# Feed-forward blocks: gated tiles turned by VectorE in 32x32 blocks, and the last down unit's low part formed by GpSimd

## The reference, cut to what matters

```python
def swiglu(x, w1, w3, w2):
    return (jax.nn.silu(x @ w1) * (x @ w3)) @ w2      # inner width 2816
```

## Time and profile before

| what | value |
|---|---|
| time, median of 3 runs | 1487.77 us (1487.43 to 1488.27) |
| profiled execution | span 1485.5 us; with what lies around it the program takes 1487.77 us in the runs above |
| TensorE busy | 1466.1 us, 99% |
| VectorE busy | 865.5 us, 58% |
| ScalarE busy | 687.0 us, 46% |
| GpSimd busy | 184.2 us, 12% |
| TensorE clock | 0.999 of full speed (mean) |

### The profile page before, as it was taken

How to read it: one execution, slowest core, us unless ns; L and a number is a source line. 1 busy time by engine, 2 the same in 40 slices (tenths; PEclk the granted TensorE clock), 3 DMA queues, 4 the chain that set the end, 5 groups by cost and what they waited for, 6 DMA issues and landing times.

```text
span 1485.5 us, 20418 instructions
## 1 busy us (share of the span) xinstructions
PE 1466.1 (99%) x7688; PEld 1237.8 (83%) x7688; DVE 865.5 (58%) x1030; ACT 687.0 (46%) x854; POOL 184.2 (12%) x184
## 2 busy tenths in 40 slices
PE   9999999999999999999999999999999999999998
PEld 8988897888888888889988888888888897788886
DVE  5765756554455545657665544675455677664545
ACT  5346446434444443453434344364434378444342
POOL 1073112000000000300040000300000325500001
PEclk9999999999999999999999999999999999999999
DMA  8744554756556655465566565576555450475561
GB/s 284 235 164 162 190 171 149 273 186 195 182 174 201 196 182 187 170 216 179 194 201 220 185 194 184 175 238 200 190 179 196 139 179 30 142 226 188 180 198 57
DMA packets 198875, 274.47 MB, mean 185 GB/s; under 512 B 9632, under 2 KB 158240, under 8 KB 198560
## 3 DMA queue, kind: packets, MB, share of 16 engines
q1 hardware_dynamic: 194304, 256.62, 53.5%
q0 software_dynamic: 4368, 16.78, 3.2%
q10 hardware_dynamic: 144, 0.26, 0.0%
HBM read 272.32 MB, written 1.31 MB: 184 GB/s over the span
## 4 chain that ended last, share of the span: by engine, by line
PE 89%; DVE 3%; POOL 3%; ACT 3%; issue 1%; DMA 1%; SPq 0%; DVEq 0%; ACTq 0%; POOLq 0%
PE ps L638 25%; PE ps L640 25%; PE ps L639 25%; PE ps L750 3%; PE ps L744 3%; PE ps L733 3%; PE ps L1066 1%; ACT whi L1427 1%; PE ps L679 1%; POOL wlo L2758 1%; DVE wlo L1995 1%; PE ps L1138 0%; PE ps L1266 0%; DMA raw<-in_w_in 0%; DVE big L2582 0%
## 5 line engine op out<-in xcount | busy, mean ns | idle before, releaser
L1995 DVE TENSOR_TENSOR wlo<-raw,whi 128x2048 fp32r<-128x2048 f32 (+1 forms) x229 | 524.3, 2292 | 319.9 <-ACT whi L1427 319.2
L1427 ACT CAST whi<-raw 128x2048 fp32r<-128x2048 f32 (+1 forms) x239 | 452.4, 1895 | 229.3 <-PE ps L640 196.2
L638 PE MATMUL ps<-whi,st_hi 128*128 128x512 f32 (+1 forms) x1064 | 419.6, 394 | 0.3 <-DVE wlo L1995 0.3
L640 PE MATMUL ps<-whi,st_lo 128*128 128x512 f32 (+1 forms) x1064 | 413.2, 388 | 0.0
L639 PE MATMUL ps<-wlo,st_hi 128*128 128x512 f32 (+1 forms) x1064 | 412.7, 388 | 0.0
L640 PEld LDWEIGHTS ps<-whi,st_lo 128*128 128x128 f32 (+1 forms) x1064 | 198.8, 187 | 41.8
L638 PEld LDWEIGHTS ps<-whi,st_hi 128*128 128x128 f32 (+1 forms) x1064 | 199.0, 187 | 39.8 <-DVE wlo L1995 0.6
L639 PEld LDWEIGHTS ps<-wlo,st_hi 128*128 128x128 f32 (+1 forms) x1064 | 199.2, 187 | 39.1
L638 PE MATMUL ps<-whi,hid_hi 128*128 128x512 f32 x400 | 156.1, 390 | 0.0
L640 PE MATMUL ps<-whi,hid_lo 128*128 128x512 f32 x400 | 155.8, 390 | 0.0
L639 PE MATMUL ps<-wlo,hid_hi 128*128 128x512 f32 x400 | 155.6, 389 | 0.0
(11 more groups left out here) (262 smaller groups left out, 1463.3 us busy)
## 6 DMA issues: line engine op xcount, KB each, us to landing
raw<-in_ffn_w SPq DMA_DIRECT2D x264, 512.0 KB, 4.3
raw<-in_w_gate_up SPq DMA_DIRECT2D x44, 512.0 KB, 4.7
raw<-in_w_in SPq DMA_DIRECT2D x32, 512.0 KB, 5.1
raw<-in_sgu_w_in SPq DMA_DIRECT2D x32, 512.0 KB, 4.6
raw<-in_w_down SPq DMA_DIRECT2D x22, 512.0 KB, 4.0
raw<-in_sgu_w_out SPq DMA_DIRECT2D x16, 512.0 KB, 4.7
raw<-in_kv_w SPq DMA_DIRECT2D x12, 512.0 KB, 4.1
raw<-in_w_proj_attn SPq DMA_DIRECT2D x8, 512.0 KB, 4.4
```

Of the source, the lines that this page charges most:

```text
L638: pe.matmul(o, a[0], b[0], start=start, stop=False)
L640: return pe.matmul(o, a[1], b[0], start=False, stop=stop)
L1427: act.copy(whi[:, s, 0:n], raw[:, s, 0:n]).then_inc(whi_ready, 1)
L1995: dve.tensor_tensor(wlo[:, s, 0:n], raw[:, s, 0:n], whi[:, s, 0:n].bitcast(F32), ALU.subtract).then_inc(wlo_ready, 1)
```

## The change

Turning leaves TensorE. VectorE copies each 32x32 block of `hidden` turned into its place of a new SBUF tile `hidT`: 16 instructions per step, each on 32 partitions x 128 elements (both token blocks), and in the last step 16 instructions of 32 x 64 elements for each token block. ScalarE's cast and VectorE's subtraction that follow read `hidT` in SBUF and not a PSUM bank. New semaphores `hid_turned` and `hid_ready` carry this; ScalarE waits for `w_used` before it overwrites `hid_hi`. In the loop the pair cast and subtraction moves behind the D unit's split. In the last step VectorE's order is: gate tb 0, turn tb 0, gate tb 1, subtract tb 0, (split of the next unit, in block 0 only), turn tb 1, subtract tb 1. The last down unit D10 of each block joins `BY_POOL`. `big` shrinks by 128 columns to make room.

```diff
@@ vector engine, swiglu
+                def turn(i, blocks=(0, 1)):
+                    for tb in blocks:
+                        dve.wait_ge(*read(("up", n, tb), i))
+                    t0, nb = blocks[0], len(blocks)
+                    for a in range(4):
+                        for b in range(4):
+                            src = view(hidden[32 * a:32 * a + 32, t0, 32 * b:32 * b + 1], (FC, nb), (P, 2), (1, 32))
+                            dst = view(hidT[32 * b:32 * b + 32, 0, P * t0 + 32 * a:P * t0 + 32 * a + 1],
+                                       (P, nb), (S, 2), (1, 32))
+                            mm = dve.transpose(dst, src)
+                    mm.then_inc(hid_turned, 1)
...
-                    dve.tensor_tensor(lo, bank(key)[:, 0:2 * P].rearrange("p (f t) -> p f t", f=2), hi.bitcast(F32),
-                                      ALU.subtract).then_inc(*is_read(key))
+                    dve.tensor_tensor(lo, hidT[:, :, tb * P:tb * P + P], hi.bitcast(F32),
+                                      ALU.subtract).then_inc(hid_ready, 1)
...
                 upto(u0 + 3)
-                hidden_out(0)
+                turn(0)
                 with dve.Fori(1, FSTEPS - 1) as i:
                     split(*at(u0 + 4, i - 1))
+                    hidden_out(i - 1)
                     split(*at(u0 + 5, i - 1))
                     hidden_in(i)
+                    turn(i)
                     split(*at(u0 + 6, i - 1))
-                    hidden_out(i)
                 nxt[0] = u0 + 3 * FSTEPS - 2
                 last = u0 + 3 * FSTEPS - 1
+                upto(last - 1)
+                hidden_out(FSTEPS - 2)
+                hidden_in(FSTEPS - 1, (0,))
+                turn(FSTEPS - 1, (0,))
                 upto(last)
-                hidden_in(FSTEPS - 1)
+                hidden_in(FSTEPS - 1, (1,))
                 hidden_last(0)
                 upto(last + 1)
+                turn(FSTEPS - 1, (1,))
                 hidden_last(1)
@@ scalar engine
                 def hidden_out(i):
-                    act.wait_ge(*full(("hid", n), i))
-                    act.copy(hid_hi[:, :, :].rearrange("p a b -> p (a b)"), bank(("hid", n))).then_inc(hi_rounded, 1)
+                    act.wait_ge(w_used, u0 + 2 + 3 * i)
+                    act.wait_ge(hid_turned, hid_count(n, i))
+                    act.copy(hid_hi[:, :, :].rearrange("p a b -> p (a b)"),
+                             hidT[:, :, :].rearrange("p a b -> p (a b)")).then_inc(hi_rounded, 1)
@@ tensor engine
-                turn(1)
                 with pe.Fori(2, FSTEPS - 1) as i:
                     gate_up(i, u0 + 2, i - 1)
                     down(i - 1, u0 + 4, i - 1)
-                    turn(i)
...
-                turn_last(0)
-                pe.wait_ge(*read(hid, i - 1))
+                pe.wait_ge(hid_ready, hid_count(n, i - 1))
...
-                turn_last(1)
@@ gpsimd engine
+        BY_POOL |= {first["ffn", n] + 3 * FSTEPS - 1 for n in range(5)}
...
+            split_last(1)
             layer_norm(("ffn", 1), first["sgv"])
```

More of the change, by code:

```diff
@@ L98, in build @@
         hidden = sb("hidden", [P, 2, FC])
+        hidT = sb("hidT", [P, 2, S])
         res = sb("res", [P, 2, D])
@@ L225, in build @@
         silu_ready = sem("silu_ready")
+        hid_turned = sem("hid_turned")
+        hid_ready = sem("hid_ready")
         zeros_ready = sem("zeros_ready")
@@ L393, in plan_ffn @@
             plan(("up", n, 1), 5, times=FSTEPS, unit=first["ffn", n] + 1)
-            plan(("hid", n), 6, split=True, times=FSTEPS - 1)
+            plan_split(("hid", n), FSTEPS - 1)
             for tb in range(2):
-                plan(("hid_last", n, tb), 6 + tb, split=True)
+                plan_split(("hid_last", n, tb))
             for tb, h in ((0, 0), (0, 1), (1, 0)):
@@ L1051, in down @@
                 def down(i, base, j, start=False):
-                    pe.wait_ge(*read(hid, i))
+                    pe.wait_ge(hid_ready, hid_count(n, i))
                     w = down_weights(base, j)
@@ L1056, in down @@
                     down_block(w, hid_hi, hid_lo, 1, start).then_inc(w_used, 1)
[L1058 to L1076, removed]
                 by_block([(u0 + half, 4, 512, 4 * half, [bank(key) for key in up], up, half == 0, half == 1)
                           for half in range(2)], st=name, src=src, beside=beside)
[L1081 to L1086, removed]
+                gate_up(1, u0 + 2, 0, between=between)
                 for key in (k for pair in ykeys for k in pair):
@@ L1702, in hidden_last @@
                 def hidden_last(tb):
[L1703 to L1706, removed]
+                    act.wait_ge(hid_turned, hid_count(n, FSTEPS - 1 + tb))
+                    act.copy(st_hi[:, 8:10, tb * P:tb * P + P], hidT[:, :, tb * P:tb * P + P]).then_inc(hi_rounded, 1)
                 def hidden_out(i):
-                    act.wait_ge(*full(("hid", n), i))
-                    act.copy(hid_hi[:, :, :].rearrange("p a b -> p (a b)"), bank(("hid", n))).then_inc(hi_rounded, 1)
+                    act.wait_ge(w_used, u0 + 2 + 3 * i)
+                    act.wait_ge(hid_turned, hid_count(n, i))
+                    act.copy(hid_hi[:, :, :].rearrange("p a b -> p (a b)"),
+                             hidT[:, :, :].rearrange("p a b -> p (a b)")).then_inc(hi_rounded, 1)
                 upto(u0 + 1)
@@ L2392, in swiglu, with hidden_in @@
                 u0 = first["ffn", n]
-                def hidden_in(i):
-                    for tb in range(2):
+                def hidden_in(i, blocks=(0, 1)):
+                    for tb in blocks:
                         dve.wait_ge(silu_ready, 2 * FSTEPS * n + tb + 1 + 2 * i)
@@ L2399, in hidden_in @@
                                           ALU.mult).then_inc(*is_read(("up", n, tb)))
+                def turn(i, blocks=(0, 1)):
+                    for tb in blocks:
+                        dve.wait_ge(*read(("up", n, tb), i))
[7 more added lines that the diff above has]
+                    mm.then_inc(hid_turned, 1)
                 def hidden_last(tb):
[L2402 to L2403 removed]
+                    dve.wait_ge(hi_rounded, split_no["hid_last", n, tb] + 1)
                     hi, lo = (x[:, 8:10, tb * P:tb * P + P] for x in (st_hi, st_lo))
[L2405 to L2406 removed]
+                    dve.tensor_tensor(lo, hidT[:, :, tb * P:tb * P + P], hi.bitcast(F32),
+                                      ALU.subtract).then_inc(hid_ready, 1)
                 def hidden_out(i):
                     dve.wait_ge(hi_rounded, split_no["hid", n] + 1 + i)
[L2410 removed]
+                    dve.tensor_tensor(hid_lo[:, :, :].rearrange("p a b -> p (a b)"),
+                                      hidT[:, :, :].rearrange("p a b -> p (a b)"),
                                       hid_hi[:, :, :].rearrange("p a b -> p (a b)").bitcast(F32),
[L2412 removed]
+                                      ALU.subtract).then_inc(hid_ready, 1)
                 upto(u0 + 2)
@@ L2870, in layer_norm, with split_last @@
                 norm_done(n)
+            def split_last(n):
+                split(first["ffn", n] + 3 * FSTEPS - 1)
+            split_last(0)
             for tb in range(2):
@@ L2929, in _ @@
             load_norm(5)
+            split_last(4)
             var_root(("ffn", 4), 0)
```

16 lines of the change are left out of this document (10 added, 6 removed).

## The result

| | before | after |
|---|---|---|
| time, median | 1487.83 us (1487.43 to 1488.27, 4 runs) | 1499.45 us (1498.6 to 1500.73, 4 runs) |
| profiled execution, span | 1485.5 us | 1499.0 us |
| granted TensorE clock, mean | 0.999 | 0.990 |

The changed kernel is 0.8% slower: ratio 1.0079, 95% interval 1.0065 to 1.0093, so +11.6 us where +9.7 was forecast.

The account below looks back on a forecast made before the run. TensorE, busy 99% of the span, was taken as the bound. Block terms -0.5 + 4.6 + 4.6 + 1.7 - 2.1 and starts +1.3 gave +9.6 us: span 1495.1, time 1497.4, rounded to 1497.5; range 1482 to 1507.

Parts of the forecast that it names:

- a turn of 16 transpositions, a half turn: VectorE's turning: 0.315 us an instruction, 5.0 us a turn; 0.25 us, 4.0 us a half turn; lower ends 3.2 and 2.1.
- starts of four blocks: VectorE's subtraction at a block's start comes 0.3 us late for TensorE in four blocks: +1.3 us in all.
- block 0: End of block 0: norm done later, +4.0 us, less 4.5 for TensorE's ten turns, a gain of 0.5.
- block 1, block 2: Ends of these blocks: TensorE's turn of `scale`'s output +9.1 us, less 4.5 for ten turns, a loss of 4.6 each.
- block 3: End of block 3: TensorE needs both halves of `scale`, +6.2 us, less 4.5, a loss of 1.7.
- block 4: End of block 4: no split behind, ends 2.4 us later, less 4.5, a gain of 2.1.
- The loop: Inside the loop nothing is late; TensorE saves 0.45 us a turn, ten turns or 4.5 us a block.
- The two stops: Ends of blocks: tb 1's subtraction stands until GpSimd's split ends at 619.8; `scale` stands behind its second split until 629.65.
- the open race: GpSimd's waiting second split gets the ports before `scale`; rival, VectorE first: 1485.0 us, chance 0.12.
- the three stops: TensorE's turn of `scale`'s output behind blocks 1, 2 and 3: +9.1, +9.1 and +6.2 us, before 4.5 off each.
- The clock: Granted clock may fall in TensorE's gaps of blocks 1 and 2: nothing taken, up to 3 us a gap for the upper end.
- GpSimd's share: GpSimd forming D10 costs nothing by itself and frees 2.2 us of VectorE ahead of the first half turn.

Follow-up runs that it names:

- the two runs on groups: Changed kernel with the transposition loops swapped, 1500.39 us; changed kernel with each transposed block written to the partitions it is read from, 1487.54 us.
- the loop's part alone: Changed kernel with the last step turned by TensorE as before and D10's low part formed by VectorE again: 1466.73 us.
- Filling two gaps: Changed kernel with eight idle fp32 matmuls of 128x512 in TensorE's gap ahead of L687 in blocks 1 and 2: 1496.55 us.
- the scale first: Changed kernel where GpSimd, behind blocks 1, 2 and 3, starts its second split only after VectorE has scaled token block 0: 1486.61 us.
- the cast first there: Changed kernel with GpSimd's wait for `scale`, plus ScalarE's next-unit cast ahead of the tb 0 cast in block 0 alone: 1485.55 us.
- the kernel with the cast first: Changed kernel with ScalarE's next-unit cast ahead of the last step's tb 0 cast: alone 1498.72 us, with GpSimd's wait for `scale` 1491.62 us.

## Why the prediction was right

The time and the mechanism held, though the closeness of the sum is in part luck: two errors of opposite sign stand behind it. The range (1482 to 1507) reached from faster to slower, so that lying in it says less than the places below. By its steps, block by block, with places of the two traces compared (the changed kernel's profiled execution was 0.8 us late after its first 13 us already, while the first weights landed; that is in no step of the kernel, and is taken off):

| step | predicted | measured |
|---|---|---|
| a turn of 16 transpositions, a half turn | 5.0, 4.0 us | 5.06, 3.99 |
| starts of four blocks | +1.3 | 1.3, in blocks 0, 1, 2 and 4; contained in the rows of the blocks |
| block 0 | -0.5 | -0.4 |
| block 1, block 2 | +4.6 each | +6.4, +5.6 |
| block 3 | +1.7 | +2.9 |
| block 4 | -2.1 | -1.9 |
| sum | +9.6 | +12.6 in this execution, +11.6 in the medians |

**The turn.** Right in size (0.316 and 0.25 us apart) and, as the two runs on groups show, in its reason; that the input's group holds as well was not in it. What bounded it from below, 0.20 us, was measured too.

**The loop.** Right: 21.5 us faster with the loop's part alone.

**The two stops.** Both where they were put: the subtraction stands 1.5 us, and `scale` behind GpSimd's second split. Whether GpSimd gets the ports before VectorE's next instruction was the open race; it did in all three blocks. In block 1 the root ends at 620.60 and the split starts with it (620.57), while `centre` still runs; `scale` starts only at 621.00. TensorE's turn came at 625.91, 4.2 us behind its place in the earlier trace rows when the 0.4 us already there at the end of block 0 are taken off; 4.9 were predicted, the late start included. Block 2 is the same (4.2 for 4.9). In block 3, again without what had gathered before, the turn came 0.25 us behind and not 1.7:

```profile
1196.09 1.97 PE L687 MATMUL ps<-con,res 128*128 128x128 f32 x8 [3.73 <-DVE res L2080]
```

There the forecast let TensorE wait for both halves of `scale`, which end at 1196.69; it began as soon as the first was there. So the three stops together were put 2.8 us too high. The wait of GpSimd for `scale` took 12.8 us off, more than the 11.6 by which the change loses. It isn't all that the last step costs: that is 32.7 us beside the loop alone.

**The clock.** The term I left at nothing, with up to 3 us a gap in the range, is the one that was mis-sized most. In all three gaps it fell to 0.50, for 4 to 6 us of work behind them; in block 1 the turn of tb 1 came 9.0 us behind that of tb 0 and not 6.7, and these 2.3 us are the step from 4.2 to 6.4. Behind tb 0's turn the three blocks lost 2.2, 1.4 and 2.7 us more, 6.2 in all. Against this stand the 2.8 us by which the stops were put too high, and 0.3 in blocks 0 and 4, so that the sum missed by 3 us in this execution and by 2 in the medians. Filling two gaps gave 2.9 us back in the medians. Block 3's gap of 3.7 us wasn't filled, so that its 2.7 us are the clock's is argued from the clock there (0.50 until 5.9 us after the turn's start) and not shown.

**GpSimd's share.** "Costs nothing by itself" held: no change beside the old last step. "Without it the place above would be that much later", 2.2 us, was wrong by far: without it GpSimd's next split falls on the first subtraction, and the program is 14.9 us slower. The sum for a moved unit has to follow the engine's next instruction, and not its own length alone.

## What to carry to other kernels

Work moved from a full engine to a half-empty one pays where the receiving engine has slack, here in the loop's steps (21.5 us), and costs where it lies on the hand-over between stages; so here the best version (1466.73 us) changes the loop and leaves the last step as it was. Where VectorE's operands move from PSUM to SBUF, list each instruction that reads two SBUF tensors and put it beside GpSimd's long ones: each can lose the whole of GpSimd's instruction (0.42 us became 4.42 here), and three of the edits here that moved GpSimd's split only moved the stop to another instruction. Where the last step has to move too, a wait that keeps GpSimd behind the one short VectorE instruction on the path gave most back (12.8 us for one wait). Two terms of a sum may also be wrong against each other: compare places inside the stretch, and not only its end.

## What the runs showed of the hardware

**A gap of TensorE costs more than itself.** In the changed kernel TensorE stands still 7.2 us in blocks 1 and 2 and 3.7 in block 3; behind each the clock was at 0.50, which is 1.2 GHz. It was back at full speed 6.0 us (block 1), 4.4 (block 2) and 5.9 (block 3) after TensorE had started again. With the scale first the gaps of blocks 1 and 2 are 3.1 us, and the clock was back 2.9 and 4.0 us after the start. So a shorter gap didn't always bring a shorter slow stretch. Behind a wait of 1.2 us (end of block 0, with the cast first there) it stayed at 1.00. At 2.64 to 2.69 us it went both ways, before the same instruction of the same code, end of block 0: it fell in the profiled executions of four kernels and not in the changed kernel's. First the changed kernel, L646 after the gap, clock 1.00:

```profile
432.11 0.50 PE L646 MATMUL ps<-whi,st_hi 128*128 128x512 f32 x1 [2.66 <-DVE st_lo L2396]
...
432.45 0.40 PE L647 MATMUL ps<-wlo,st_hi 128*128 128x512 f32 x1
432.68 0.40 PE L648 MATMUL ps<-whi,st_lo 128*128 128x512 f32 x1
```

Then the kernel with the scale first, which is the same code up to there:

```profile
431.53 0.79 PE L646 MATMUL ps<-whi,st_hi 128*128 128x512 f32 x1 [2.64 <-DVE st_lo L2396]
432.12 0.63 PE L647 MATMUL ps<-wlo,st_hi 128*128 128x512 f32 x1
432.55 0.63 PE L648 MATMUL ps<-whi,st_lo 128*128 128x512 f32 x1
```

There the starts are 0.43 us apart and not 0.23, and the first turn behind them comes 1.1 us later for it. That this place also makes executions of one kernel differ by about a microsecond is likely, but one profile of each kernel doesn't show it.

**The ports are lost both ways.** In the kernel with the cast first, GpSimd's split of block 1 took 5.16 us and not 4.5, beginning within VectorE's pair and standing until that had ended:

```profile
621.30 1.42 DVE L2080 SCALAR_TENSOR_TENSOR res<-tmp,rstd,gb 128x512 f32<-128x512 f32 x2
...
622.06 5.16 POOL L2756 TENSOR_TENSOR wlo<-raw,whi 128x2048 fp32r<-128x2048 f32 x1 [1.16 <-ACT whi L1405]
```

In block 2 of the same execution the split came 0.03 us behind the pair's recorded start (957.23 against 957.20), ran in 4.49, and the pair took 5.74. So with the split 0.76 us behind the pair's start it was the split that stood, and with 0.03 it was VectorE; 4.3 us of the pair hang on it. Where between the two the turning point lies isn't shown. Gating (one PSUM and one SBUF tensor, 0.42 us at 604.59 in the changed kernel) and the transpositions (3.99 and 3.98 us), beside splits of GpSimd, kept their lengths.
